# Query variance in one matmul a block after an add on GpSimd, and the key look-up of both key sets in half precision

## The chip, the cores and the metric

One core of a Trainium2 chip runs the whole program. The metric is the device time of one execution in microseconds (us), the median of several runs. The engines are TensorE (PE in the profile, with PEld for its weight loads), VectorE (DVE), ScalarE (ACT), GpSimd (POOL) and SyncE (SP), which issues most of the transfers.

## What is computed

The reference is one layer of a network on 512 tokens of 1024 numbers: a layer norm, an adaptive modulation, a mixer (pooling and a linear recurrence), and a product-key expert layer (PEER). The change lies in the choice of experts:

```python
q = (hf @ w_q).reshape(T, PEER_HEADS, PEER_DKEY)
q = (q - mean(q)) * rsqrt(var(q) + LN_EPS)
s1 = einsum('thd,nd->thn', q[..., :half], k1)
s2 = einsum('thd,nd->thn', q[..., half:], k2)
v1, i1 = top_k(s1, 16)
v2, i2 = top_k(s2, 16)
cand = (v1[..., :, None] + v2[..., None, :]).reshape(T, 8, 256)
vs, j = top_k(cand, 16)
e = i1[j // 16] * 128 + i2[j % 16]
g = softmax(vs)
out = einsum('tk,tkd->td', g * gelu(einsum('td,tkd->tk', x, u[e])), v[e])
```

There are 8 heads with a query of 256 numbers each, two sets of 128 keys, and 16 x 16 candidates of which 16 are kept. The kernel centres the query weights beforehand, so the variance of a query is the mean of its 256 squares.

## The kernel before, in words

All 128 x 128 experts are computed densely for the first 384 tokens (three of four blocks of 128), as 128 tiles of 128 experts: each tile is 24 matmuls of 384 columns (lines 982 to 984, the helper `thrice`, which splits each factor in a high and a low part and multiplies three times). The weights of the chosen experts are scattered into a dense gate. The last 128 tokens gather their rows instead.

The order of work is written out by hand, engine by engine, and semaphores tie the engines together. Around the change it is as follows.

**Queries.** TensorE makes the query of a head in two halves of 24 matmuls each, `queries(h)`. ScalarE reads each half out of its bank twice, as a copy `qT` (line 790) and as a square `sq` (line 791). Once the matmuls of head h+1 are issued, TensorE makes `scores` of head h: 8 matmuls of queries by keys (line 1126), then the variance (line 1130): for each of 4 blocks, two matmuls of one column, the two halves of the squares by a column of 1/256, summed in the bank. In the trace each of these matmuls is two records. ScalarE then reads the scores out (line 802).

**Queue of GpSimd in this stage.** For each head it makes the low parts of two weight pieces (`lo_weights`, line 574), from the fourth head on behind a centring of weights (`centre`, line 592). Then follow the low parts of the expert tiles (`split_u`, line 616, two instructions a tile), of which tiles 2 to 17 come with a scale or a shift of the residual (`affine`, lines 566 and 569).

**Routing on VectorE.** `route(h)` does, per head and in order: the 16 largest of both score lists in 4 blocks (lines 1586 to 1597), a cast of their positions (line 1615), the candidate sums, the 16 largest candidates, integer work that gives the two places `ka` and `kb` of each choice (lines 1625 to 1632), and the look-up of the keys at these places (lines 1634 to 1641): two comparisons with 0 to 15, two products with the positions, two sums over 16. Each of these six works on 128 x 1024 single-precision numbers. `step` links a result to the next instruction by a semaphore. The eight heads follow one another without a pause, and the softmax follows them.

**The turn.** TensorE works on expert tiles 0 to 34 meanwhile. In tile 34, after 6 of its 8 chunks, it waits for the softmax (`s_wt`) and for all keys (`s_e1e2`) and transposes them for the scatter (line 1184, 9 transposes). ScalarE's exponential (line 843) stands in its queue behind the readout of tile 32; GpSimd waits for the picks of the last block before the low part of tile 35. Then TensorE finishes tile 34, does tile 35, and begins 24 scatter steps (lines 1195 and 1197), each with one expert tile. In these VectorE makes the half-precision one-hot tables (lines 1692 and 1698) and the low part of the tile (line 1685).

Of the kernel before, what the change touches and what calls it, by code (L numbers as in the profile page):

```python
# [8 lines left out]
F16 = mybir.dt.float16  # L9
U32 = mybir.dt.uint32  # L10
I32 = mybir.dt.int32
ACT = mybir.ActivationFunctionType
AX = mybir.AxisListType


P = 128
D = 1024
KD = D // P
S = 512
TB = S // P  # L20
# [7 lines left out]
H = 8  # L28
DK = 256
NK = 128  # L30
K = 16
PICKS = H * K
# [94 lines left out]
def build(nc, x, cols, rows, consts, ada_w, w_in, w_out, wq, pool_w, wa, wx, k1t, k2t, ut, u, v, out):  # L127
    ctx = ExitStack()
    with ctx:
# [3 lines left out]
        def sem(name):  # L133
            return ctx.enter_context(nc.semaphore(name))
# [77 lines left out]
        def carve(spec):  # L212
            at, got = 0, []
            for shape in spec:
# [26 lines left out]
        (qT, sq, keys, e1, e2, wt, vs, s_all, s_val, s_pos, s_posf, cand, c_val, c_idx, dec, eq_a, eq_b,  # L241
# [3 lines left out]
             (TB * K, K), (TB * K, K), (4, TB * H)])  # L245

# [72 lines left out]
        s_fin = [sem(f"output{n}_ready") for n in range(TB)]  # L319
        s_wthi, s_wtlo = sem("weights_hi_ready"), sem("weights_lo_ready")  # L320
# [223 lines left out]
        def _(pool):  # L544
# [58 lines left out]
            pool.dma_start(keys[:, 1, :], k2t).then_inc(s_keys, 16)  # L603
            for h in range(1, H):
                if h == 4:
                    pool.wait_ge(s_centre, 4)
                if h >= 4:
                    centre(h)
                if h > 1:
                    lo_weights(NZ + 2 * h)  # L610
                lo_weights(NZ + 2 * h + 1)

# [7 lines left out]
            split_u(0, 1)  # L620
            pool.wait_ge(s_wtlo, NZ + 2 * H)
# [317 lines left out]
        def _(pe):  # L939
# [178 lines left out]
            def scores(par, h, first, var_at):  # L1118

                pe.wait_ge(s_qev, h * 2 + 2)  # L1120
                if not first:
                    pe.wait_ge(s_sev, h * 2 - 2)
                for tb in range(TB):
                    for half in range(2):
                        at = (tb % 2) * DK + half * NK
                        pe.matmul(bank[(2, 5)[par] + tb // 2][:, at:at + NK],
                                  qT[:, par, half, tb * P:(tb + 1) * P], keys[:, half, :], start=True, stop=True)
                for tb in range(TB):
                    for half in range(2):
                        mm = pe.matmul(bank[4][:, var_at(tb)], sq[:, par, half, tb * P:(tb + 1) * P], mean_col,  # L1130
                                       start=(half == 0), stop=(half == 1))
                mm.then_inc(s_smm, 1)
# [151 lines left out]
        def _(ve):  # L1284
# [317 lines left out]
            ka, kb, low = dec[:, 4, :], dec[:, 5, :], dec[:, 6, :]  # L1602
            iota16 = iota[:, 0:K].unsqueeze(1).to_broadcast([P, TB * K, K])
# [3 lines left out]
            def route(h):  # L1607
# [5 lines left out]
                last.then_inc(s_routed, 1)  # L1613
                ve.wait_ge(s_routed, h + 1)
                ve.tensor_copy(s_posf, s_pos.bitcast(U32))
# [18 lines left out]
                ve.tensor_tensor(eq_b, kb.unsqueeze(2).to_broadcast([P, TB * K, K]), iota16, ALU.is_equal)  # L1634
                step(ve.tensor_tensor(eq_a, ka.unsqueeze(2).to_broadcast([P, TB * K, K]), iota16, ALU.is_equal))  # L1635
                ea = eq_a.rearrange("p (t j) a -> p t j a", t=TB)
                eb = eq_b.rearrange("p (t j) a -> p t j a", t=TB)
                ve.tensor_tensor(ea, ea, s_posf[:, 0].unsqueeze(2).to_broadcast([P, TB, K, K]), ALU.mult)  # L1638
                step(ve.tensor_tensor(eb, eb, s_posf[:, 1].unsqueeze(2).to_broadcast([P, TB, K, K]), ALU.mult))  # L1639
                ve.tensor_reduce(e1[:, :, h * K:(h + 1) * K], ea, AX.X, ALU.add)  # L1640
                ve.tensor_reduce(e2[:, :, h * K:(h + 1) * K], eb, AX.X, ALU.add).then_inc(s_e1e2, 1)
# [150 lines left out]
            for c in range(split, early_end):  # L1792
                split_u(0, c)
                n = c - split
# [156 lines left out]
```

## Time and profile before

| what | value |
|---|---|
| median of 3 runs | 1442.37 us (1441.28 to 1442.58) |
| time of the profiled execution | 1443.12 us |
| its span | 1441.3 us |
| PE busy | 1412.3 us, 98% of the span |
| DVE busy | 1239.7 us, 86% |
| ACT busy | 589.5 us, 41% |
| POOL busy | 556.1 us, 39% |
| mean granted clock of TensorE | 0.989 |
| chain that ended last, by engine | PE 70%, DVE 24%, DMA 2%, ACT 2%, issue 1% |

The span is that of one profiled execution, from its first to its last instruction; 1.8 us of that execution's time lie outside it. The chain is followed back from the last instruction, at each step to what released it. A busy engine may still hold others up or be held up for a few microseconds, and such places are found in the waits and in the timeline of an engine.

### The profile page before, as it was taken

The page shows a single profiled execution, that of the slowest core. Times are in us where ns is not written, and L with a number is a line of the kernel's source. Part 1 is how long each engine was busy: PE and PEld are TensorE (multiplying, and loading weights), DVE is VectorE, ACT ScalarE, POOL GpSimd, SP SyncE. Part 2 cuts the span into 40 slices and gives each one's busy share as a digit, 9 for nine tenths or more (in the row PEclk, how much of TensorE's full clock was granted, in tenths as well). Part 3 has the DMA queues.
Part 4 walks back from the last instruction along what each step waited for, and adds up shares of the span by engine and source line. Part 5 has one row for each costly group of instructions (what it writes and reads, how often), then busy time and mean ns, then how long its engine had stood idle before and what let it go on. Part 6 is the DMA issues. An engine that isn't in the chain of part 4 may idle for free.

```text
span 1441.3 us, 20694 instructions
## 1 busy us (share of the span) xinstructions
PE 1412.3 (98%) x7503; PEld 1234.6 (86%) x7503; DVE 1239.7 (86%) x2019; ACT 589.5 (41%) x693; POOL 556.1 (39%) x389
## 2 busy tenths in 40 slices
PE   7999989999998999999999999999999999999997
PEld 6775478899998999998888888888888888888886
DVE  6988969999998999756888888888798888888889
ACT  3561263333334888843333333333333333333331
POOL 0100224549864000002445555454456555554500
PEclk7899999999999999999999999999999999999999
DMA  9824450025565799998999999999999999999961
GB/s 382 326 117 175 146 193 1 1 76 167 174 224 168 263 284 301 290 350 332 371 355 353 375 355 370 355 367 367 349 374 367 371 356 369 381 356 367 353 227 59
DMA packets 159566, 402.34 MB, mean 279 GB/s; under 512 B 11632, under 2 KB 79344, under 8 KB 156432
## 3 DMA queue, kind: packets, MB, share of 16 engines
q1 hardware_dynamic: 120928, 262.17, 51.7%
q0 software_dynamic: 38288, 139.08, 25.4%
q8 instruction: 34, 0.56, 0.2%
q10 hardware_dynamic: 288, 0.29, 0.1%
q14 instruction: 28, 0.23, 0.0%
HBM read 359.56 MB, written 41.94 MB: 279 GB/s over the span
## 4 chain that ended last, share of the span: by engine, by line
PE 70%; DVE 24%; DMA 2%; ACT 2%; issue 1%; SPq 0%; DVEq 0%; ACTq 0%
PE bank L982 22%; PE bank L983 22%; PE bank L984 21%; DVE arena L1597 2%; DVE arena L1589 2%; DMA wbuf<-ada_w_dram 2%; PE bank L1195 2%; PE bank L1197 2%; DVE arena L1594 1%; DVE arena L1586 1%; DVE arena L1638 1%; DVE arena L1591 1%; DVE arena L1639 1%; PE bank L1071 1%; DVE arena L1635 1%
## 5 line engine op out<-in xcount | busy, mean ns | idle before, releaser
L982 PE MATMUL bank<-h_lo,u_hi 128*128 128x384 f32 (+1 forms) x1256 | 438.9, 349 | 2.0 <-POOL u_lo L616 1.9
L983 PE MATMUL bank<-h_hi,u_lo 128*128 128x384 f32 (+1 forms) x1256 | 433.4, 345 | 0.0
L984 PE MATMUL bank<-h_hi,u_hi 128*128 128x384 f32 (+1 forms) x1256 | 433.4, 345 | 0.0
L983 PE MATMUL bank<-v_hi,w_lo 128*128 128x512 f32 x744 | 294.6, 396 | 0.0
L982 PE MATMUL bank<-v_lo,w_hi 128*128 128x512 f32 x744 | 292.1, 393 | 0.3 <-DVE w_lo L1735 0.3
L984 PE MATMUL bank<-v_hi,w_hi 128*128 128x512 f32 x744 | 290.4, 390 | 0.0
L982 PEld LDWEIGHTS bank<-h_lo,u_hi 128*128 128x128 f32 x1256 | 236.5, 188 | 14.0 <-ACT arena L819 2.2
L876 ACT ACTIVATE v_hi<-v_raw 128x2048 fp32r<-128x2048 f32 x62 | 119.0, 1919 | 311.7 <-PE bank L984 301.7
L983 PEld LDWEIGHTS bank<-h_hi,u_lo 128*128 128x128 f32 x1256 | 236.5, 188 | 11.3 <-issue 0.5
L984 PEld LDWEIGHTS bank<-h_hi,u_hi 128*128 128x128 f32 x1256 | 236.3, 188 | 9.5
L1729 DVE TENSOR_TENSOR v_lo<-v_raw,v_hi 128x2048 fp32r<-128x2048 f32 x62 | 142.8, 2303 | 110.5 <-ACT v_hi L876 109.0
L811 ACT ACTIVATE u_hi<-u_raw 128x1024 fp32r<-128x1024 f32 x128 | 135.2, 1057 | 126.2 <-PE bank L984 126.2
L641 POOL DMA_INDIRECT quad<-v_dram,pick_at x86 | 130.7, 1520 | 114.2 <-DVE picked L1756 98.0
L641 POOL DMA_INDIRECT quad<-u_dram,pick_at x84 | 118.0, 1405 | 129.7 <-DVE quad L1748 87.4
L982 PEld LDWEIGHTS bank<-v_lo,w_hi 128*128 128x128 f32 x744 | 139.7, 188 | 32.1 <-DVE w_lo L1735 0.6
L984 PEld LDWEIGHTS bank<-v_hi,w_hi 128*128 128x128 f32 x744 | 139.8, 188 | 31.5
L983 PEld LDWEIGHTS bank<-v_hi,w_lo 128*128 128x128 f32 x744 | 139.6, 188 | 28.3
L641 POOL DMA_INDIRECT first_rows<-u_dram,pick_at x44 | 60.3, 1371 | 252.8 <-DVE w_raw L1722 177.9
L1685 DVE TENSOR_TENSOR u_lo<-u_raw,u_hi 128x1024 fp32r<-128x1024 f32 x92 | 112.2, 1220 | 21.3 <-ACT u_hi L811 15.8
L616 POOL TENSOR_TENSOR u_lo<-u_raw,u_hi 128x512 fp32r<-128x512 f32 x72 | 103.4, 1457 | 46.5 <-ACT u_hi L811 40.3
L1756 DVE SCALAR_TENSOR_TENSOR picked<-quad,pick_g,picked 128x1024 f32<-128x1024 f32 x86 | 110.0, 1279 | 1.6
L1748 DVE SCALAR_TENSOR_TENSOR quad<-quad,h_nat 128x1024 f32<-128x1024 f32 x84 | 101.9, 1219 | 0.0
(246 smaller groups left out, 1815.1 us busy)
## 6 DMA issues: line engine op xcount, KB each, us to landing
u_raw<-ut_dram SPq DMA_DIRECT2D x128, 512.0 KB, 5.7
v_raw<-v_dram SPq DMA_DIRECT2D x64, 1024.0 KB, 7.2
gate_in<-gates_dram SPq DMA_DIRECT2D x64, 384.0 KB, 7.2
wbuf<-ada_w_dram SPq DMA_DIRECT2D x6, 2048.0 KB, 11.3
early_dram<-arena SPq DMA_DIRECT2D x64, 192.0 KB, 2.4
gates_dram<-wbuf SPq DMA_DIRECT2D x12, 1024.0 KB, 7.1
gates_dram<-arena SPq DMA_DIRECT2D x12, 1024.0 KB, 7.4
w_raw<-early_dram SPq DMA_DIRECT2D x64, 192.0 KB, 5.3
```

What stands on the lines that cost most here:

```text
L616: pool.tensor_tensor(u_lo[:, c % GT, ks], u_raw[:, c % RT, ks], u_hi[:, c % GT, ks].bitcast(F32), ALU.subtract).then_inc(done, 1)
L641: pool.indirect_dma_start(row_buf(n), None, of, bass.IndirectOffsetOnAxis(ap=pick_at[:, k:k + 1], axis=0)).then_inc(s_rows_of[n % NBUF], 16)
L811: act.activation(u_hi[:, c % GT], u_raw[:, c % RT], ACT.Copy).then_inc(s_uhi, 1)
L876: act.activation(v_hi[:, c % 2], v_raw[:, c % 2 * 2:c % 2 * 2 + 2, :], ACT.Copy).then_inc(s_vhi, 1)
L982: pe.matmul(out, a_hi, b_lo, start=(k == 0), stop=False)
L983: pe.matmul(out, a_lo, b_hi, start=False, stop=False)
L984: return pe.matmul(out, a_hi, b_hi, start=False, stop=(k == n - 1))
L1195: pe.matmul(bank[q][:, t * P:(t + 1) * P], onehot[b][:, 1, pair, :, at], gate[b][:, 0, pair, :, at], start=True, stop=False)
L1685: ve.tensor_tensor(u_lo[:, c % GT], u_raw[:, c % RT], u_hi[:, c % GT].bitcast(F32), ALU.subtract).then_inc(s_ulo, 1)
L1729: ve.tensor_tensor(v_lo[:, c % 2], v_raw[:, c % 2 * 2:c % 2 * 2 + 2, :], v_hi[:, c % 2].bitcast(F32), ALU.subtract).then_inc(s_vlo, 1)
L1748: ve.scalar_tensor_tensor(out=rows_of, in0=rows_of, scalar=1.0, in1=h_nat[:, :], op0=ALU.mult, op1=ALU.mult, accum_out=dots[:, k:k + 1]).t ...
L1756: ve.scalar_tensor_tensor(out=picked[:, :], in0=rows_of, scalar=pick_g[:, k:k + 1], in1=picked[:, :], op0=ALU.mult, op1=ALU.add).then_inc( ...
```

## The change

Two edits. In the first, GpSimd adds the two halves of a head's squares in place (`sum_squares`), and TensorE makes the variance of each block with one matmul instead of two, behind a new semaphore. In the second, the look-up of the keys of both sets is done together on half-precision numbers laid out in pairs: one comparison and one product on 2048 numbers, then three adds that halve the list of 16 (1024, 512 and 256 numbers), and a last add (128 numbers) that writes single precision. The arrays `e1` and `e2` lie side by side and are written through one view, `e_both`.

```diff
+        e_both = arena[:, 2 * 2 * S + 2 * 2 * S + 2 * NK:][:, 0:2 * TB * PICKS].rearrange("p (m n) -> p m n", m=2 * TB)
...
+            def sum_squares(h):
+
+                pool.wait_ge(s_qev, 2 * h + 2)
+                pool.tensor_tensor(sq[:, h % 2, 0], sq[:, h % 2, 0], sq[:, h % 2, 1], ALU.add).then_inc(s_sqsum, 1)
+
             for h in range(1, H):
...
                 lo_weights(NZ + 2 * h + 1)
+                sum_squares(h - 1)
...
             split_u(0, 0)
             split_u(0, 1)
+            sum_squares(H - 1)
             pool.wait_ge(s_wtlo, NZ + 2 * H)
...
+                pe.wait_ge(s_sqsum, h + 1)
                 for tb in range(TB):
-                    for half in range(2):
-                        mm = pe.matmul(bank[4][:, var_at(tb)], sq[:, par, half, tb * P:(tb + 1) * P], mean_col,
-                                       start=(half == 0), stop=(half == 1))
+                    mm = pe.matmul(bank[4][:, var_at(tb)], sq[:, par, 0, tb * P:(tb + 1) * P], mean_col,
+                                   start=True, stop=True)
...
-            ka, kb, low = dec[:, 4, :], dec[:, 5, :], dec[:, 6, :]
-            iota16 = iota[:, 0:K].unsqueeze(1).to_broadcast([P, TB * K, K])
+            ka, kb, low = (dec[:, 4, :].bitcast(F16)[:, 0:TB * K], dec[:, 4, :].bitcast(F16)[:, TB * K:], dec[:, 6, :])
+            lists, pairs = 2 * TB, K // 2
+            place_of = dec[:, 4, :].bitcast(F16)
+            place = place_of.rearrange("p (g t) -> p g t", t=2)
+            place_key = dec[:, 7, 0:K].bitcast(F16).rearrange("p (a t) -> p a t", t=2)
+            pos_twice = pos_at.rearrange("p a t k -> p (a t k)").bitcast(F16).rearrange("p (a t) -> p a t", t=2)
+            found, told = (a.rearrange("p n k -> p (n k)").bitcast(F16).rearrange("p (g a t) -> p g a t", a=K, t=2)
+                           for a in (eq_a, eq_b))
...
+                if h == 0:
+                    ve.tensor_copy(place_key, iota[:, 0:K].unsqueeze(2).to_broadcast([P, K, 2]))
                 ve.wait_ge(s_routed, h + 1)
-                ve.tensor_copy(s_posf, s_pos.bitcast(U32))
+                ve.tensor_copy(pos_twice, s_pos.rearrange("p a t k -> p (a t k)").bitcast(U32).unsqueeze(2)
+                               .to_broadcast([P, lists * K, 2]))
...
-                ve.tensor_tensor(eq_b, kb.unsqueeze(2).to_broadcast([P, TB * K, K]), iota16, ALU.is_equal)
-                step(ve.tensor_tensor(eq_a, ka.unsqueeze(2).to_broadcast([P, TB * K, K]), iota16, ALU.is_equal))
-                ea = eq_a.rearrange("p (t j) a -> p t j a", t=TB)
-                eb = eq_b.rearrange("p (t j) a -> p t j a", t=TB)
-                ve.tensor_tensor(ea, ea, s_posf[:, 0].unsqueeze(2).to_broadcast([P, TB, K, K]), ALU.mult)
-                step(ve.tensor_tensor(eb, eb, s_posf[:, 1].unsqueeze(2).to_broadcast([P, TB, K, K]), ALU.mult))
-                ve.tensor_reduce(e1[:, :, h * K:(h + 1) * K], ea, AX.X, ALU.add)
-                ve.tensor_reduce(e2[:, :, h * K:(h + 1) * K], eb, AX.X, ALU.add).then_inc(s_e1e2, 1)
+                step(ve.tensor_tensor(found, place.unsqueeze(2).to_broadcast([P, lists * pairs, K, 2]),
+                                      place_key.unsqueeze(1).to_broadcast([P, lists * pairs, K, 2]), ALU.is_equal))
+                step(ve.tensor_tensor(told.rearrange("p (m j) a t -> p m j (a t)", m=lists),
+                                      found.rearrange("p (m j) a t -> p m j (a t)", m=lists),
+                                      pos_twice.rearrange("p (m a) t -> p m (a t)", m=lists).unsqueeze(2)
+                                      .to_broadcast([P, lists, pairs, 2 * K]), ALU.mult))
+                for w in (K // 2, K // 4, K // 8):
+                    step(ve.tensor_tensor(told[:, :, 0:w], told[:, :, 0:w], told[:, :, w:2 * w], ALU.add))
+                ends = [told[:, :, n, :].rearrange("p (m j) t -> p m j t", m=lists) for n in range(2)]
+                ve.tensor_tensor(e_both[:, :, h * K:(h + 1) * K].rearrange("p m (j t) -> p m j t", t=2),
+                                 ends[0], ends[1], ALU.add).then_inc(s_e1e2, 1)
```

Two places show how the queues stand. The line numbers are each program's own. On GpSimd, from the first low weight piece behind the key loads to the first expert tiles, before (`u_lo<-wbuf` is a low weight piece, `wbuf<-wbuf,hmean` a centring, `u_lo<-u_raw` a low expert tile):

```order
23 L574 TENSOR_TENSOR u_lo<-wbuf,u_hi 128x1024 x5
24 L592 TENSOR_TENSOR wbuf<-wbuf,hmean 128x8x256
25 L574 TENSOR_TENSOR u_lo<-wbuf,u_hi 128x1024 x2
...
30 L592 TENSOR_TENSOR wbuf<-wbuf,hmean 128x8x256
31 L574 TENSOR_TENSOR u_lo<-wbuf,u_hi 128x1024 x2
32 L616 TENSOR_TENSOR u_lo<-u_raw,u_hi 128x512 x6
33 L566 TENSOR_TENSOR xt<-xt,row_g 128x512
```

and now (`arena<-arena` of line 610 is the add of the squares):

```order
23 L577 TENSOR_TENSOR u_lo<-wbuf,u_hi 128x1024
24 L610 TENSOR_TENSOR arena<-arena 128x512
25 L577 TENSOR_TENSOR u_lo<-wbuf,u_hi 128x1024 x2
26 L610 TENSOR_TENSOR arena<-arena 128x512
27 L577 TENSOR_TENSOR u_lo<-wbuf,u_hi 128x1024 x2
28 L610 TENSOR_TENSOR arena<-arena 128x512
29 L595 TENSOR_TENSOR wbuf<-wbuf,hmean 128x8x256
...
39 L577 TENSOR_TENSOR u_lo<-wbuf,u_hi 128x1024 x2
40 L610 TENSOR_TENSOR arena<-arena 128x512
41 L625 TENSOR_TENSOR u_lo<-u_raw,u_hi 128x512 x4
42 L610 TENSOR_TENSOR arena<-arena 128x512
43 L625 TENSOR_TENSOR u_lo<-u_raw,u_hi 128x512 x2
```

An add of the squares stands behind the second weight piece of each head, ahead of the next centring; the last stands behind the low parts of expert tiles 0 and 1.

On VectorE, the look-up of one head with the instruction ahead of it, before (names in brackets are the semaphores waited for):

```order
224 L1632 TENSOR_TENSOR arena<-arena 128x64 [waits route_step]
225 L1634 TENSOR_TENSOR arena<-arena,cst 128x1024 [waits route_step]
226 L1635 TENSOR_TENSOR arena<-arena,cst 128x1024
227 L1638 TENSOR_TENSOR arena<-arena 128x1024 [waits route_step]
228 L1639 TENSOR_TENSOR arena<-arena 128x1024
229 L1640 TENSOR_REDUCE arena<-arena 128x4x16 [waits route_step]
230 L1641 TENSOR_REDUCE arena<-arena 128x4x16
```

and now (the size is that of the output):

```order
225 L1651 TENSOR_TENSOR arena<-arena 128x64 [waits route_step]
226 L1653 TENSOR_TENSOR arena<-arena 128x2048 [waits route_step]
227 L1655 TENSOR_TENSOR arena<-arena 128x2048 [waits route_step]
228 L1660 TENSOR_TENSOR arena<-arena 128x64x16 [waits route_step]
229 L1660 TENSOR_TENSOR arena<-arena 128x64x8 [waits route_step]
230 L1660 TENSOR_TENSOR arena<-arena 128x64x4 [waits route_step]
231 L1662 TENSOR_TENSOR arena<-arena 128x8x16 [waits route_step]
```

Six instructions stand for six; all of the new ones have two inputs, and each waits for the one ahead of it.

## Rows read from the trace of the kernel before

**Rows 1.** The page, part 1: busy us, share of span, instructions.
```profile
PE 1412.3 (98%) x7503; PEld 1234.6 (86%) x7503; DVE 1239.7 (86%) x2019; ACT 589.5 (41%) x693; POOL 556.1 (39%) x389
```

**Rows 2.** Waits of PE: line, releaser: us in total, times, longest us.
```profile
PE bank L1184 <- issue: 3.6, 1, 3.6
PE bank L982 <- POOL u_lo L616: 1.9, 1, 1.9
```

**Rows 3.** Timeline of PE, variance of heads 0 and 6: start us, us, instruction.
```profile
213.77 1.84 PE L1130 MATMUL bank<-cst,arena 128*128 128x1 f32 x16
215.48 0.49 PE L982 MATMUL bank<-h_lo,u_hi 128*128 128x512 f32 x1
...
300.85 1.84 PE L1130 MATMUL bank<-cst,arena 128*128 128x1 f32 x16
302.79 0.41 PE L982 MATMUL bank<-h_lo,u_hi 128*128 128x384 f32 x1
```

**Rows 4.** Timeline of POOL, queries to tiles, and tiles with affine.
```profile
274.68 3.61 POOL L592 TENSOR_TENSOR wbuf<-wbuf,hmean 128x2048 f32<-128x2048 f32 x1
...
286.86 2.37 POOL L574 TENSOR_TENSOR u_lo<-wbuf,u_hi 128x1024 fp32r<-128x1024 f32 x1 [2.97 <-ACT u_hi L697]
301.37 5.02 POOL L616 TENSOR_TENSOR u_lo<-u_raw,u_hi 128x512 fp32r<-128x512 f32 x4 [12.14 <-ACT u_hi L811]
308.52 2.60 POOL L616 TENSOR_TENSOR u_lo<-u_raw,u_hi 128x512 fp32r<-128x512 f32 x2 [2.13 <-ACT u_hi L811]
...
349.47 4.36 POOL L616 TENSOR_TENSOR u_lo<-u_raw,u_hi 128x512 fp32r<-128x512 f32 x2 [0.37 <-ACT u_hi L811]
353.79 2.27 POOL L569 TENSOR_TENSOR xt<-xt,row_b 128x512 f32<-128x512 f32 x1
356.02 3.50 POOL L616 TENSOR_TENSOR u_lo<-u_raw,u_hi 128x512 fp32r<-128x512 f32 x2
```

**Rows 5.** Chain that ended last, look-ups of heads 2 and 7: start us, us, what.
```profile
290.97 1.23 DVE arena L1634
...
296.98 1.12 DVE arena L1641
...
442.32 1.23 DVE arena L1634
...
451.49 1.13 DVE arena L1641
```

**Rows 6.** Groups by line, DVE: busy us, mean ns | idle us.
```profile
L1692 DVE TENSOR_TENSOR arena<-arena 128x2048 f16<-128x2048 f16 x24 | 28.4, 1221 | 0.0
L1615 DVE CAST arena<-arena 128x128 f32<-128x128 uint32 x8 | 2.5, 313 | 0.3
```

**Rows 7.** Timeline of PE at the turn.
```profile
452.83 0.33 PE L983 MATMUL bank<-h_hi,u_lo 128*128 128x384 f32 x1
453.00 0.34 PE L984 MATMUL bank<-h_hi,u_hi 128*128 128x384 f32 x1
...
457.80 1.54 PE L1184 MATMUL bank<-cst,arena 128*128 128x128 f32 x6 [0.35 <-ACT arena L819]
...
465.14 0.24 PE L1195 MATMUL bank<-arena 128*128 128x128 f16 x1
...
467.01 0.44 PE L982 MATMUL bank<-h_lo,u_hi 128*128 128x384 f32 x1
```

**Rows 8.** Windows: us, busy us (instructions) PE, PEld, DVE, ACT, POOL; PEclk, DMA, GB/s.
```profile
458.00:464.00 6.00, 6.00 (x30) 6.00 (x30) 3.94 (x5) 2.54 (x6) 3.06 (x4) 0.77 0.69 206
```

**Rows 9.** Timeline of ACT at the turn.
```profile
447.63 1.28 ACT L843 ACT_TABLE_LOAD   x1
454.37 0.63 ACT L843 ACTIVATE arena<-arena 128x512 f32<-128x512 f32 x1 [5.45 <-DVE arena L1657]
```

**Rows 10.** Timeline of DVE behind the turn.
```profile
459.95 0.36 DVE L1676 CAST arena<-arena 128x384 f16<-128x384 f32 x1 [2.53 <-ACT arena L852]
...
465.74 1.22 DVE L1685 TENSOR_TENSOR u_lo<-u_raw,u_hi 128x1024 fp32r<-128x1024 f32 x1
```

More of the change, by code:

```diff
@@ L239, in build @@
         part = arena[:, ARENA - 2 * CHUNK_C:].rearrange("p (b n) -> p b n", b=2)
-        (qT, sq, keys, e1, e2, wt, vs, s_all, s_val, s_pos, s_posf, cand, c_val, c_idx, dec, eq_a, eq_b,
+        (qT, sq, keys, e1, e2, wt, vs, s_all, s_val, s_pos, pos_at, cand, c_val, c_idx, dec, eq_a, eq_b,
          pk) = carve(
@@ L245, in build @@
              (TB * K, K), (TB * K, K), (4, TB * H)])
+        e_both = arena[:, 2 * 2 * S + 2 * 2 * S + 2 * NK:][:, 0:2 * TB * PICKS].rearrange("p (m n) -> p m n", m=2 * TB)
+        assert 2 * TB * K * K == 2 * (TB * K * K)
         s_of = ([s_all[:, 0], s_all[:, 1], arena[:, ARENA - TB * DK:].rearrange("p (t n) -> p t n", t=TB), s_all[:, 2]]
@@ L319, in build @@
         s_fin = [sem(f"output{n}_ready") for n in range(TB)]
+        s_sqsum = sem("query_squares_summed")
         s_wthi, s_wtlo = sem("weights_hi_ready"), sem("weights_lo_ready")
```

## Prediction

> **What bounds the kernel now.** I read the page's busy shares first: TensorE is busy for 98% of the span [rows 1]. Only two things can then shorten the run: less work on TensorE, or fewer of its few idle microseconds. Its waits show two that matter here: 3.6 us in front of the transposes of the turn, and 1.9 us for a low expert tile from GpSimd [rows 2]. The chain of waits says what stands behind the first. VectorE's routing is on it for all eight heads, and the last look-up ends at 451.49 + 1.13 = 452.62 us [rows 5]. ScalarE's exponential waits 5.45 us for the shifted values [rows 9] and TensorE waits for the softmax after that. So routing is late by a few microseconds against tile 34, and nowhere else in front of the turn does TensorE wait for it. Behind the turn TensorE is full again to within a few microseconds, so time won before it stays won.
>
> **The variance on TensorE.** One head's 16 records take 215.48 - 213.77 = 1.71 us [rows 3]. Half of them goes: 0.86 us a head. For seven heads that is 6.0 us off the path. For head 6 I count nothing. Its 16 records stand ahead of expert tile 0, and the next matmul starts 302.79 - 300.85 = 1.94 us after the first of them, 0.23 us later than for head 0: the low part of tile 0, which GpSimd began at 301.37 us, is already what it waits for [rows 3, 4], and the edit does not speed that up. Bounds: 5.1 us if another head loses its share, 6.9 us if all eight count.
>
> **The add on GpSimd.** Eight instructions of 128 x 512 with two inputs. The nearest row is the low expert tile, 5.02 / 4 = 1.26 us each [rows 4]. I cost them at nothing on the path, for these covers. From variance to variance a head takes (300.85 - 213.77) / 6 = 14.5 us [rows 3]. GpSimd has two weight pieces of 2.4, a centring of 3.6 and now 1.3 us in it, 9.7 us [rows 4]. The squares of head 6 are added behind the piece that ends at 286.86 + 2.37 = 289.23 us, so by about 290.5 us, and their variance begins at 300.85 us: 10 us to spare [rows 3, 4]. Queued behind each add are the next centring and the next weight piece, which come 1.3 us later; the pieces' idle of about 3 us for ScalarE [rows 4] takes most of that up. The last add falls into the 2.13 us that GpSimd waits ahead of tile 2 [rows 4]. If the cover were gone, the price would be 1.26 us a head.
>
> **The look-up on VectorE.** Alone, in head 2, the old six take from 290.97 to 298.10 us, 7.1 us; in head 7, among GpSimd's instructions, from 442.32 to 452.62 us, 10.3 us [rows 5]. For the new ones, the half-precision one-hot tables have the same shape and pairing: 2048 numbers in 1.22 us [rows 6], so 2.44 us for comparison and product. The three adds and the last one have no row. Below lies the rate of the tables without a fixed part, (1024 + 512 + 256 + 128) / 2048 x 1.22 = 1.1 us; above lies one number in 1.2 ns, that of the comparison [rows 5], with the 0.31 us of the cast of 128 numbers as the floor of each [rows 6], 2.5 us. I take a line between table and cast, 0.73 + 0.49 + 0.37 + 0.31 = 1.9 us, since the first two are nearest to the tables. Sum 4.3 us, a saving of 2.8 us in a head that is alone. The cast of positions doubles, at most 0.3 us more [rows 6], and one small cast comes once. That leaves at least 2.5 x 8 = 20 us over the heads.
>
> How much is needed? TensorE and with it ScalarE come to the turn 6.0 us earlier, and the values are 5.45 us late now [rows 9], so 11.5 us; 0.86 us comes from routing beginning earlier. The need is 10.6 us, 1.3 us a head. I expect it met, and what is over is worth nothing: ScalarE takes the exponential behind tile 32 whatever comes earlier.
>
> **The turn.** With the softmax there, TensorE goes on after 453.17 us (in the times of before) with 9 transposes at about 0.107 us (the pace of the variance's records, the nearest row [rows 3]) and 6 + 24 matmuls at 0.17 us [rows 7]: 453.17 + 1.0 + 5.1 = 459.3 us for the first scatter matmul, which came at 465.14 us [rows 7]. So 5.9 us are lost now: the waits, and matmuls at the low clock, since the granted clock was 0.77 in the 6 us behind the wait [rows 8]. What is late next is VectorE's preparation of the scatter. From the second lot of transposes at 457.80 us to its first cast at 459.95 us lie 2.15 us, and 7.06 us more to the matmul at 467.01 us that needs its low part of tile 36 [rows 7, 10]. Starting the second lot at about 453.5 us gives 453.5 + 2.15 + 7.06 = 462.7 us instead of 467.01: **4.3 us won**, 1.6 given back. I take 4.3; the upper bound is 5.9.
>
> **GpSimd among the expert tiles.** In tiles 2 to 17 it makes a low tile and an affine piece per tile, 3 x 1.26 = 3.8 us of TensorE's 24 x 0.17 = 4.1 us. In head 4's look-up its instructions stretched to 4.36, 2.27 and 3.50 us where 2.5, 1.3 and 2.5 are usual [rows 4], 3.8 us in all, and TensorE's 1.9 us of waiting came of it [rows 2]. The new look-up holds GpSimd for about as long (4.3 us against the old four two-input instructions' 4 x 1.15), but heads come closer together and two may fall into this stage. Bounds: 1.9 us won if none does, 3.8 us lost if two more do. I take 1.0 us lost.
>
> **Sum.** 6.0 + 4.3 - 1.0 = 9.3 us. The profiled execution took 1443.12 us (span 1441.3 and 1.8 around it), so its like would take 1433.8; against the median of 1442.37 us, 0.8 below that execution, **1433.1 us**.
>
> **Rivals.**
> First, more: GpSimd's wait vanishes and the scatter's preparation keeps up. 6.0 + 5.9 + 1.9 = 13.8 us, 1428.6 us. For it speaks that the add instructions are short; against it that heads 3 to 5 still meet the busy stage.
>
> Second, GpSimd becomes the bound among the expert tiles. All six new look-up instructions have two inputs, where two of the old six were sums with one. If three heads fall into tiles 2 to 17 and each costs TensorE what a stretch of 3.8 us less 0.9 of slack costs, 2.9 us, the wait is 8.7 us for 1.9: 6.0 + 4.3 - 6.8 = 3.5 us won, 1438.9 us. For it speak the stretched rows [rows 4]; against it that the same total of VectorE time is held.
> The Trainium skill, "SBUF — State Buffer", section "Who interferes with whom", states that VectorE instructions with two SBUF inputs and GpSimd instructions that read SBUF shut each other out for a whole instruction. The stretched rows agree. By that rule alone every new instruction may stand behind one of GpSimd's.
> Six waits of 1.26 us on 4.3 us would make a look-up 11.9 us, longer than the 10.3 us of before, where GpSimd never rests; with at most three such heads and 2.5 us saved in the five others, 12.5 - 4.8 = 7.7 us are saved where 10.6 are needed, and the turn would keep about 3 us of its wait. I leave that inside this rival's time.
>
> Third, the half-precision look-up is no faster. At one number in 1.12 ns, 2048 take 2.3 us, the six 2 x 2.3 + 2.5 = 7.1 us, just what the old take. Then VectorE ends where it did but for 0.86 us, and all that TensorE saves is spent waiting at the turn: 1441.5 us, no change. Against it stand the tables' 1.22 us [rows 6].
> The Trainium skill, "Vector Engine (DVE) Microarchitecture Reference", section "Performance modes", reports that a two-source instruction on 2-byte numbers fell to the single rate when one input re-read one element as its innermost step. Here the innermost step is a pair of neighbours, as in the tables, whose row shows the double rate; by the rule the place to look is the last add, whose output is single precision.
>
> Fourth, slower: the new wait in front of the variance. If the squares come late, TensorE stands with the next head's queries queued behind. It decides once an add ends after the eight key matmuls; each head would then pay an add held by a VectorE instruction, 1.26 + 1.15 = 2.4 us, 19.3 us over the eight, against 6.9 + 4.3 won: 8 us lost, 1450.5 us. For it speaks only that the add is queued behind two weight pieces; against it stand 10 us of slack.
>
> **How the numbers follow.** Forecast 0.66, more 0.11, GpSimd as the bound 0.14, no faster look-up 0.06, late squares 0.03. The range 1428.5 to 1438.0 holds the forecast with its bounds (6.9 + 5.9 - 1.0 = 11.8 us won; 5.1 + 4.3 - 3.8 = 5.6 us won), the better case and half of the second rival. About 0.2% (2.9 us) is what a measurement can tell from no change: faster is below 1439.5 us. That is the forecast, the better case and some 0.10 of the second rival, 0.87; no change is its rest and the third, 0.10; slower is 0.03.
>
> **What would show it.** Right: 64 records of the variance at about 0.86 us a head with no idle before them; the look-up at 4 to 5 us alone; the exponential without its 5.45 us of waiting; the granted clock near 1 behind the turn; scatter starting 10 to 11 us earlier; a wait for GpSimd's low tiles of 1 to 4 us. Wrong: an idle TensorE in front of the variance, a comparison of over 2 us in a head that is alone, or the waits for low tiles above 6 us.

## The result: 1446.7 us, slower by 4.4

The changed kernel takes 1446.69 us (median of 8 runs, 1446.05 to 1448.23), the kernel before 1442.32 us beside it (8 runs, 1441.13 to 1443.39): a ratio of 1.0033, 95% interval 1.0024 to 1.0041. The forecast of 1433.1 us and its range to 1438.0 us are missed, and on the other side.

In the lines of the changed kernel the comparison of a look-up is line 1653, the product 1655, the three adds 1660, the last add 1662; on GpSimd a weight piece is line 577, the add of the squares 610, a centring 595. The page's part 1, which answers to [rows 1]:

```profile
PE 1405.0 (97%) x7439; PEld 1226.1 (85%) x7439; DVE 1244.5 (86%) x2020; ACT 590.0 (41%) x693; POOL 563.4 (39%) x397
```

TensorE does 32 matmuls less (64 records, two to a matmul) and is busy 7.3 us less, and yet the span grew from 1441.3 to 1444.7 us. Its waits (columns as in [rows 2]) say where this went:

```profile
PE bank L1194 <- DVE arena L1684: 14.2, 1, 14.2
...
PE bank L992 <- POOL u_lo L625: 1.7, 3, 1.0
```

The timeline of TensorE at the turn, and below it that of ScalarE:

```profile
445.68 0.34 PE L994 MATMUL bank<-h_hi,u_hi 128*128 128x384 f32 x1
460.21 2.41 PE L1194 MATMUL bank<-cst,arena 128*128 128x128 f32 x9 [14.19 <-DVE arena L1684]
```

```profile
440.31 1.28 ACT L853 ACT_TABLE_LOAD   x1
457.64 0.63 ACT L853 ACTIVATE arena<-arena 128x512 f32<-128x512 f32 x1 [16.05 <-DVE arena L1679]
```

TensorE comes to the turn at 446.0 us, 7.3 us earlier than before [rows 7], where the variance had promised 6.0, and stands there for 14.2 us. The exponential waits 16.05 us, where it waited 5.45 [rows 9]. Routing is taken here from the first maximum of head 0 to the instruction behind the last look-up. Its two ends in the kernel before, and below them now:

```profile
216.77 1.65 DVE L1586 MAX8 arena<-arena 128x8 f32<-128x128 f32 x8 [10.20 <-ACT arena L802]
...
452.54 0.34 DVE L1651 RECIPROCAL arena<-arena 128x32 f32<-128x32 f32 x1
```

```profile
215.67 1.65 DVE L1596 MAX8 arena<-arena 128x8 f32<-128x128 f32 x8 [8.06 <-ACT arena L812]
...
455.81 0.35 DVE L1673 RECIPROCAL arena<-arena 128x32 f32<-128x32 f32 x1
```

It ends 3.3 us later, and the span is 3.4 us longer. All that TensorE won is spent waiting for VectorE.

Routing did not lose time everywhere. By VectorE's timeline (a head begins with its first maximum) the first four heads, which run beside the projection of the queries and the first expert tiles, took 127.9 us in place of 108.7; the last four 112.2 in place of 127.1. So the question is what held VectorE in the first four heads. The chain that ended last, in the look-up of head 0 (start, us, what):

```profile
236.06 1.24 DVE arena L1653
...
237.32 3.31 DVE arena L1655
...
240.65 0.70 DVE arena L1660
...
241.38 2.64 DVE arena L1660
...
244.04 1.28 DVE arena L1660
...
245.34 3.58 DVE arena L1662
```

and GpSimd's timeline in the same microseconds:

```profile
236.08 3.45 POOL L577 TENSOR_TENSOR u_lo<-wbuf,u_hi 128x1024 fp32r<-128x1024 f32 x1 [1.17 <-ACT u_hi L707]
241.33 2.40 POOL L577 TENSOR_TENSOR u_lo<-wbuf,u_hi 128x1024 fp32r<-128x1024 f32 x1 [1.80 <-ACT u_hi L707]
243.68 1.48 POOL L610 TENSOR_TENSOR arena<-arena 128x512 f32<-128x512 f32 x1
245.12 3.65 POOL L595 TENSOR_TENSOR wbuf<-wbuf,hmean 128x2048 f32<-128x2048 f32 x1
```

Each of VectorE's held instructions ends just behind one of GpSimd's. The product comes out 1.1 us, a little under its own 1.24, behind the end of the first piece (239.53 us), which the comparison had held back in its turn; the second add 0.3 us behind the second piece (244.02 and 243.73), the third 0.2 us behind the add of the squares (245.32 and 245.16), and the last add, 128 results, 0.15 us behind the centring (248.92 and 248.77). Head 7's look-up runs while TensorE stands and GpSimd is out of work, and shows what the same six cost alone:

```profile
451.57 1.24 DVE arena L1653
...
452.83 1.24 DVE arena L1655
...
454.09 0.70 DVE arena L1660
...
454.82 0.44 DVE arena L1660
...
455.28 0.30 DVE arena L1660
...
455.60 0.29 DVE arena L1662
```

From 451.57 to 455.81 us are 4.24 us, against 12.78 for head 0. Over all eight heads (instructions by line: duration in ns, min/median/max, first and last start):

```profile
L1655 DVE TENSOR_TENSOR arena<-arena x8: 1225/2200/3295, 237.3 to 452.8; 128x2048 f16<-128x2048 f16 x8
```

```profile
L1660 DVE TENSOR_TENSOR arena<-arena x24: 292/1270/2756, 240.7 to 455.3; 128x1024 f16<-128x1024 f16 x8, 128x512 f16<-128x512 f16 x8, 128x256 f16<-128x256 f16 x8
```

```profile
L1662 DVE TENSOR_TENSOR arena<-arena x8: 293/1263/3579, 245.3 to 455.6; 128x128 f32<-128x128 f16 x8
```

An add that takes 0.29 us alone takes 1.26 us in the middle of the cases and 3.58 at worst. That is not its own work but the length of one whole instruction of GpSimd (1.26, 2.4 or 3.6 us). The sums with one input that the old look-up ended with, in the kernel before:

```profile
L1641 DVE TENSOR_REDUCE arena<-arena x8: 1208/1209/1210, 243.9 to 451.4; 128x64 f32<-128x1024 f32 x8
```

were held in no head.

### The profile page after: what moved, and what is told of

It is laid out like the page before. It is cut to its first block, busy times and chain, and to the rows that moved or that the text cites. A ratio compares the mean times of both kernels' runs of the same rounds, so it can differ in the third digit from the quotient of the medians.

```text
span 1444.7 us, 20575 instructions
## 1 busy us (share of the span) xinstructions
PE 1405.0 (97%) x7439; PEld 1226.1 (85%) x7439; DVE 1244.5 (86%) x2020; ACT 590.0 (41%) x693; POOL 563.4 (39%) x397
## 4 chain that ended last, share of the span: by engine, by line
PE 70%; DVE 24%; DMA 2%; ACT 2%; issue 1%; SPq 0%; DVEq 0%; ACTq 0%
PE bank L992 22%; PE bank L993 21%; PE bank L994 21%; DVE arena L1660 2%; DVE arena L1607 2%; DVE arena L1599 2%; DMA wbuf<-ada_w_dram 2%; PE bank L1205 2%; PE bank L1207 2%; DVE arena L1604 1%; DVE arena L1596 1%; DVE arena L1655 1%; DVE arena L1601 1%; DVE arena L1653 1%; PE bank L1081 1%
## 5 line engine op out<-in xcount | busy, mean ns | idle before, releaser
L992 PEld LDWEIGHTS bank<-h_lo,u_hi 128*128 128x128 f32 x1256 | 236.4, 188 | 14.2 <-issue 1.5
L993 PEld LDWEIGHTS bank<-h_hi,u_lo 128*128 128x128 f32 x1256 | 236.5, 188 | 11.3 <-issue 0.5
```

The costliest lines, as they stand in the source:

```text
L992: pe.matmul(out, a_hi, b_lo, start=(k == 0), stop=False)
L993: pe.matmul(out, a_lo, b_hi, start=False, stop=False)
```

## The experiments

Theory H: VectorE's instructions with two inputs and GpSimd's hold each other for a whole instruction; the new look-up has six such for four, and the adds of the squares put more of GpSimd's in their way. Rivals: the halves of the change lose by something of their own (late squares, a slow operation), or the start of routing against GpSimd's rhythm decides by chance.

Read from the traces of the main kernels: routing as above, the sum of its eight look-ups, and what is held, which is routing less 8 times a head that is alone (24.0 us with the old look-up, 21.2 with the new, 21.7 with one sum). Each routing time is that of one profiled execution; the ratio is to the kernel before taken beside each.

| kernel | routing us | look-ups us | held us | time us | ratio to before, 95% |
|---|---|---|---|---|---|
| before | 235.8 | 74.2 | 43.8 | 1442.3 | |
| after | 240.1 | 71.2 | 70.5 | 1446.7 | 1.0024 to 1.0041 |
| variance part alone | 247.9 | 85.2 | 55.9 | 1455.1 | 1.0066 to 1.0100 |
| look-up part alone | 227.9 | 55.7 | 58.3 | 1436.3 | 0.9940 to 0.9973 |
| after, one sum for the adds | 207.8 | 46.9 | 34.2 | 1429.7 | 0.9890 to 0.9923 |

**The variance part alone** (the old look-up):

```diff
+                sum_squares(h - 1)
...
-                    for half in range(2):
-                        mm = pe.matmul(..., sq[:, par, half, ...], mean_col, start=(half == 0), stop=(half == 1))
+                    mm = pe.matmul(..., sq[:, par, 0, ...], mean_col, start=True, stop=True)
```

> The first edit alone: GpSimd adds the squares and TensorE makes the variance with one matmul a block; the look-up is the old one. Theory A (routing on VectorE ends last at the turn, and an instruction of VectorE that reads two arrays stands behind a running GpSimd instruction): the adds put more GpSimd work beside routing, the old look-up has four instructions that can be held, and what TensorE saves is spent waiting at the turn. Routing about 236 us long as before, give or take 3, time 1440 to 1445 us. Theory B (the adds on GpSimd are what made the change slower, the look-up helps): routing 243 us or longer, time above 1447 us.

**The look-up part alone** (the change without the add of the squares, with the two matmuls a block):

```diff
-                sum_squares(h - 1)
...
-                    mm = pe.matmul(..., sq[:, par, 0, ...], mean_col, start=True, stop=True)
+                    for half in range(2):
+                        mm = pe.matmul(..., sq[:, par, half, ...], mean_col, start=(half == 0), stop=(half == 1))
```

> The second edit alone: the half-precision look-up of both key sets; the variance is the old one. Theory A: the six instructions with two inputs are held as often as GpSimd runs, so routing is not shorter than before by more than 4 us, and may be longer; time 1438 to 1446 us. Theory B (the look-up helps, the adds hurt): routing shorter by 15 us or more, the wait at the turn gone, time below 1438 us.

Measured: the variance part loses 12 us by itself, as theory B said, and the look-up part wins 6. Theory A fell in both runs. Of the look-up part theory B had the time and the turn right, but routing fell by 7.9 us where B wanted 15: the new look-up helps, and is held more all the same. TensorE's wait at the turn in the variance part alone:

```profile
PE bank L1192 <- DVE arena L1670: 19.2, 1, 19.2
```

In the look-up part alone no wait stands ahead of the 9 transposes of the turn (line 1186 there); what is left is 0.7 us further on, ahead of a scatter matmul (line 1197) that waits for VectorE's one-hot tables:

```profile
451.66 1.14 PE L1186 MATMUL bank<-cst,arena 128*128 128x128 f32 x9
...
457.88 0.24 PE L1197 MATMUL bank<-arena 128*128 128x128 f16 x1
```

```profile
PE bank L1197 <- DVE arena L1712: 0.7, 1, 0.7
```

With these two look-ups the effects add up: the variance part brings routing 12.1 us with the old one (235.8 to 247.9) and 12.2 with the new (227.9 to 240.1). It is no fixed price, though, as a run below with another look-up shows. The look-up part saves 22.4 us of work alone (8 times 2.8) and is held 14.5 us more, so 7.9 us of routing are left.

**One sum for the four adds** (the change, with the whole sum over 16 places in one instruction with one input):

```diff
-                for w in (K // 2, K // 4, K // 8):
-                    step(ve.tensor_tensor(told[:, :, 0:w], told[:, :, 0:w], told[:, :, w:2 * w], ALU.add))
-                ve.tensor_tensor(e_both[...], ends[0], ends[1], ALU.add).then_inc(s_e1e2, 1)
+                ve.tensor_reduce(e_both[...].rearrange("p m (j t) -> p m j t", t=2),
+                                 told.rearrange("p (m j) a t -> p m j t a", m=lists), AX.X, ALU.add).then_inc(s_e1e2, 1)
```

> The change with its three adds and the last add replaced by one sum over 16 with one input, 2048 numbers, some 2.2 us by the old sums' 1.21 us for 1024. Alone the look-up is then 1.22 + 1.22 + 2.2 = 4.7 us, longer than the 4.3 us of the change. Theory A: only two instructions of the look-up can be held, so it takes 5 to 8 us in each head where the change took 8 to 13, routing ends 15 to 25 us earlier than in the change, the exponential does not wait, and the time is 1432 to 1437 us. Theory C (the length of the instructions decides, holds are the same whatever the count): no better than the change, 1446 us or more.

Alone this look-up is longer (4.72 us for 4.24), and yet routing falls by 32.3 us, to 207.8, and the time to 1429.67 us (ratio 0.9907). Both are better than theory A allowed; theory C fell. The sum's row, and TensorE's waits (line 1205 is a scatter matmul):

```profile
L1659 DVE TENSOR_REDUCE arena<-arena x8: 2285/2286/2287, 241.1 to 421.7; 128x128 f32<-128x2048 f16 x8
```

```profile
PE bank L992 <- POOL u_lo L625: 1.0, 1, 1.0
...
PE bank L1205 <- DVE arena L1717: 0.7, 1, 0.7
```

Eight records within 2 ns of each other, in the same stage in which four short adds took up to 3.6 us each; no wait for the softmax is left. H holds here, and this version beats both kernels. The same again:

> The change with one sum over 16, taken again beside the runs above and in five rounds, as the version that beat both kernels: 1428.5 to 1431 us, ratio to the kernel before 0.990 to 0.992 by every theory that takes routing off the path.

1430.24 us, ratio 0.9911 (0.9894 to 0.9927); routing again took 207.8 us.

**One add, then the sum over 8 places:**

```diff
+                step(ve.tensor_tensor(told[:, :, 0:K // 2], told[:, :, 0:K // 2], told[:, :, K // 2:], ALU.add))
-                                 told.rearrange(...)
+                                 told[:, :, 0:K // 2].rearrange(...)
```

> The change with its first add kept (1024 numbers, 0.70 us alone) and one sum over the 8 left in place of the other three adds (1024 numbers, 1.21 us). Alone 1.22 + 1.22 + 0.70 + 1.21 = 4.35 us. Theory A: three instructions can be held in place of six, routing 10 to 20 us shorter than in the change and up to 8 us longer than with the one sum; the turn's wait is gone all the same, 1432 to 1438 us. Theory C: as the change, 1446 us.

Routing 212.5 us, 4.7 more than with the one sum, for one instruction that can be held; that is 27.6 us less than in the change, more than theory A's 20. The time, 1430.40 us (0.9896 to 0.9929), doesn't show the 4.7, since routing is off the path by then.

**The one sum with the old variance:**

> The look-up with one sum over 16 and the old variance, no adds on GpSimd. With the adds this look-up gave 1429.7 us and no wait at the turn. Theory A: routing is shorter still without the adds (200 us or less by their 12 us elsewhere), but nothing waits for it, and TensorE has its 16 records a head back: 1434 to 1438 us, 5 to 7 us slower than with the adds. Rival (the sum is what wins, the variance edit gives nothing on TensorE): 1429 to 1431 us.

Routing 204.7 us; 1436.76 us (0.9938 to 0.9972). Against 1429.7 to 1430.2 with the variance in one matmul, that part is worth 6.5 to 7.1 us, once routing is off the path, so the rival fell. Routing was to be 200 us or less and is not: with this look-up the variance part brings it 3.1 us (204.7 to 207.8), not 12.

The rest asks why the variance part holds routing by 12 us with the other two look-ups. **The adds without TensorE's gain** (the variance part alone, with the summed squares multiplied twice):

```diff
+                    for half in range(2):
+                        mm = pe.matmul(bank[4][:, 64 * half:][:, var_at(tb)], sq[:, par, 0, ...], mean_col, ...)
```

> The old look-up, GpSimd's adds of the squares as in the first edit, but TensorE does as much as before: of its two matmuls a block one makes the variance and the other a copy of it in columns that nothing reads. Theory A1 (the adds themselves, 1.29 us each behind a weight piece and ahead of a centring, hold routing): routing is 245 to 250 us as with the first edit alone (247.9), time 1450 to 1456 us. Theory A2 (what hurts is that a faster TensorE moves the weight pieces and centrings closer together and under other parts of routing): routing 234 to 239 us, time 1440 to 1445 us.

Routing 236.8 us, 1444.0 us (0.9998 to 1.0017): the adds alone cost 1.0 us of routing.

**TensorE's gain without the adds** (the kernel before with the first half of the squares alone; the second is left out of the variance):

> The old look-up, no adds on GpSimd, and one matmul a block: the variance is made of the first half of the squares alone, the second half is left out. Theory A1: routing as before (236 us, give or take 3), TensorE waits longer at the turn, time 1439 to 1443 us. Theory A2: routing 245 us or longer, time above 1449 us.

Routing 232.2 us, 1438.72 us (0.9965 to 0.9984): this costs routing nothing either. Theory A1 fell in the run before, A2 in this one: only both together cost the 12 us.

**A later start.** One, two or four sums over 1024 numbers ahead of head 0's routing, in the changed kernel, and two in the variance part alone:

```diff
+                for _ in range(N if h == 0 else 0):
+                    step(ve.tensor_reduce(dec[:, 6, 0:1], s_all[:, 0].rearrange("p t n -> p (t n)"), AX.X, ALU.add))
```

> The whole change, with one idle sum (1024 numbers, one input, about 1.2 us) on VectorE ahead of the first head's routing, so that routing starts 1.2 us later against GpSimd's pieces. Theory P (how long routing takes hangs on which of its two-input instructions fall on GpSimd's runs of weight piece, add and centring, so it moves by several microseconds with the start): routing without the idle sum changes from 240.1 us by 3 us or more, up or down; time anywhere from 1436 to 1452 us. Theory S (each edit brings a fixed sum of holds): routing 240 us give or take 1.5, time 1.2 us above the change, 1446.5 to 1449 us.

> As the run before with two idle sums, 2.4 us. Theory P: another routing time, 3 us or more from 240.1 or from the run before. Theory S: time 2.4 us above the change, 1448 to 1450 us.

> With four idle sums, 4.8 us. Theory P: at least one of the three delays makes the run faster than the change itself, though VectorE does more; this one 1438 to 1455 us. Theory S: 4.8 us above the change, 1450 to 1453 us.

> The first edit alone (old look-up, GpSimd's adds, 1455.1 us, routing 247.9 us) with two idle sums, 2.4 us, ahead of the first head's routing. Theory P: the 12 us that adds and faster TensorE cost together, while neither alone cost more than 1.5, are a matter of alignment and part by 3 us or more: 1445 to 1452 us, or above 1460. Theory S: 2.4 us later, 1456.5 to 1459 us.

Routing took 238.8, 241.3 and 238.5 us for 240.1, and 251.8 for 247.9; the times were 1446.09, 1450.55, 1450.18 and 1460.85 us (1.0018 to 1.0037, 1.0039 to 1.0073, 1.0038 to 1.0071 and 1.0109 to 1.0142). Neither theory came out as written. In the changed kernel routing moved by less than the 3 us that theory P wanted, and the 0.6 us by which one delay was faster lie within the spread of the runs. In the variance part alone it moved by 3.9 us, to above 1460, as P said. Theory S fell there, and in the changed kernel the delays of 1.2, 2.4 and 4.8 us came out as 0.6 us less, 3.9 and 3.5 us more. So the start is worth up to 4 us of routing, and differences below that should not be read as a cause. But none of these starts gave the 12 us back, and two of the four made routing longer.

**The add between the weight pieces**, instead of behind both:

```diff
+                sum_squares(h - 1)
                 lo_weights(NZ + 2 * h + 1)
-                sum_squares(h - 1)
```

> The variance part alone (old look-up), with the add of the squares queued between the two weight pieces of a head instead of behind them, so that GpSimd's longest row without a pause is add and piece (3.7 us) and piece and centring (6.0 us, as in the kernel before), not 7.3 us. Theory B (a row of piece, add and centring without a pause is what holds routing): routing falls from 247.9 to at most 240 us, the time from 1455 to 1447 us or less. Theory L (the load on GpSimd in a shorter turn of the heads counts, wherever the add stands): routing 245 to 250 us, 1453 to 1457 us.

Routing 247.9 us, 1453.48 us (1.0052 to 1.0086): where the add stands among the pieces doesn't matter to routing. Theory B fell, L's figures came true.

**Adds of half the length:**

> The variance part alone (old look-up) with adds of 256 of the 512 columns (the second halves of the other columns' squares are left out): 0.65 us for 1.29. Theory L (load): routing in the middle between that with no adds and TensorE as fast, 232.2, and that with whole adds, 247.9: 238 to 242 us. Theory B (a row without a pause): the row is 6.6 us for 7.3, so most of the loss stays, 244 us or more. Theory J (chance of the alignment): anything from 230 to 250 us without order.

Routing 236.8 us, 1443.66 us (0.9990 to 1.0011). B fell again, and it is less than L said: beside TensorE's gain alone (232.2 us) whole adds cost 15.7 us of routing and half adds 4.6, so the loss doesn't grow evenly with the load.

**Short centrings**, in the variance part alone, in the kernel before, and in the whole change:

```diff
-                pool.tensor_tensor(w, w, hmean[:, h, :].unsqueeze(2).to_broadcast([P, KD, DK]), ALU.add
+                pool.tensor_tensor(w[:, 0:1], w[:, 0:1], hmean[:, h, 0:1].unsqueeze(2).to_broadcast([P, 1, DK]), ALU.add
```

> The variance part alone (old look-up) with centrings of 256 columns in place of 2048: 7 of 8 key chunks of the query weights stay without their mean. A centring then takes about 0.7 us for 3.6. If the 3.6 us centrings are what the adds and the shorter turn make routing meet more often, routing is within 3 us of the kernel before with the same short centrings; if they are not, it stays 8 us or more above it.

> The kernel before with centrings of 256 columns in place of 2048 (7 of 8 key chunks of the query weights stay without their mean): the mate of the run ahead of it. Routing falls from 235.8 us by 2 to 10 us, since 2.9 us of GpSimd a head go; the time follows by at most 6 us, what the turn waits.

> The whole change, with centrings of 256 columns in place of 2048 (7 of 8 key chunks of the query weights stay without their mean). With the old look-up the short centrings took the variance part's loss of 12.1 us of routing away but for 0.4 us. Theory C (adds, a faster TensorE and 3.6 us centrings hold routing only together): routing is as with the new look-up alone, 227.9 us, less what short centrings bring by themselves, 4 us: 222 to 229 us, and the time 1432 to 1437 us. Rival N (the six two-input instructions of the new look-up are held whatever the centrings): routing 235 us or more, 1440 us or more.

GpSimd's row of the variance part alone, one turn of the heads, with whole centrings and then with short ones:

```profile
230.05 1.29 POOL L608 TENSOR_TENSOR arena<-arena 128x512 f32<-128x512 f32 x1
231.30 3.61 POOL L593 TENSOR_TENSOR wbuf<-wbuf,hmean 128x2048 f32<-128x2048 f32 x1
236.07 3.45 POOL L575 TENSOR_TENSOR u_lo<-wbuf,u_hi 128x1024 fp32r<-128x1024 f32 x1 [1.17 <-ACT u_hi L705]
```

```profile
230.11 1.29 POOL L608 TENSOR_TENSOR arena<-arena 128x512 f32<-128x512 f32 x1
231.36 0.62 POOL L593 TENSOR_TENSOR wbuf<-wbuf,hmean 128x256 f32<-128x256 f32 x1
236.00 2.99 POOL L575 TENSOR_TENSOR u_lo<-wbuf,u_hi 128x1024 fp32r<-128x1024 f32 x1 [4.03 <-ACT u_hi L705]
```

The pause behind the centring grows from 1.17 to 4.03 us, and routing takes 232.1 us with the adds (1437.98 us, 0.9950 to 0.9980) and 231.7 without (1439.23 us, 0.9965 to 0.9991): of 12.1 us of loss 0.4 are left. In the whole change routing takes 222.6 us in place of 240.1, and the time is 1430.91 us (0.9888 to 0.9945), 1 us below the range of theory C; rival N is out. The turn's wait of 14.2 us is gone, and what is left is the wait ahead of a scatter matmul:

```profile
PE bank L1205 <- DVE arena L1720: 0.7, 1, 0.7
```

So the runs show that the variance part's loss, with the old look-up, needs three things at once: GpSimd's whole adds, the shorter turn of the heads on TensorE (13.6 us for 14.5), and centrings of 3.6 us. Take any one away and routing is within 1.1 us of the same kernel without the variance part, or below it.

What stays open is the step from these three to the 12 us. GpSimd's two pauses in a turn (in brackets) shrink. In the kernel before they are 3.2 and 2.8 us; in the variance part alone the first is 1.2 us, as shown above, and the second 1.8. The kernel before, then the variance part alone:

```profile
237.94 2.57 POOL L574 TENSOR_TENSOR u_lo<-wbuf,u_hi 128x1024 fp32r<-128x1024 f32 x1 [3.19 <-ACT u_hi L697]
243.32 2.38 POOL L574 TENSOR_TENSOR u_lo<-wbuf,u_hi 128x1024 fp32r<-128x1024 f32 x1 [2.81 <-ACT u_hi L697]
```

```profile
241.31 2.81 POOL L575 TENSOR_TENSOR u_lo<-wbuf,u_hi 128x1024 fp32r<-128x1024 f32 x1 [1.78 <-ACT u_hi L705]
```

The pauses don't decide it by themselves: with the one sum they are the same 1.2 and 1.8 us, and the loss is 3.1. By heads, the variance part alone loses 11.8 us in heads 0 and 1, among the weight pieces, and 11.3 in heads 2 and 3, and the last four give 10.9 back. For the second share the traces offer a reason. Between its last work for the queries and the first expert tile GpSimd pauses for 12.1 us in the kernel before and for 9.9 in the variance part alone. In the kernel before, head 2's look-up begins in that pause, at 290.97 us, and nothing holds it [rows 4, 5]. In the variance part alone, heads 0 and 1 being late, it begins at 303.12 us, when the pause is over and GpSimd is among the expert tiles:

```profile
284.62 1.28 POOL L608 TENSOR_TENSOR arena<-arena 128x512 f32<-128x512 f32 x1
295.79 5.04 POOL L623 TENSOR_TENSOR u_lo<-u_raw,u_hi 128x512 fp32r<-128x512 f32 x4 [9.89 <-ACT u_hi L819]
```

```profile
303.12 2.21 DVE L1642 TENSOR_TENSOR arena<-arena,cst 128x1024 f32<-128x1024 f32 x1
```

In each of the seven runs whose routing is more than 2 us longer than in the kernel before, head 2's look-up begins behind this pause; in all others it begins before the pause ends. That is read from the traces and not shown, since no run moved head 2's look-up alone, and why heads 0 and 1 lose their 11.8 us only with all three together stays unexplained.

## Why the prediction was wrong, and where it was right

**Wrong: the look-up's saving.** "At least 2.5 x 8 = 20 us over the heads ... I expect it met." The alone price was right: 4.24 us in head 7 for the 4.3 worked out, comparison and product 1.24 us each for 1.22. But a look-up was alone in one head of eight; the sum went from 74.2 to 71.2 us, 3.0 saved where 20 were counted and 10.6 needed. Without the variance part it fell to 55.7, and 7.9 us of routing were won. The step took the saving of a head that is alone, 2.8 us, for every head. Yet its own row of head 7 [rows 5] already showed 3.2 us of holding on four instructions that can be held, and the new look-up offers six.

**Wrong: the add on GpSimd at nothing.** "I cost them at nothing on the path, for these covers." The covers are those of TensorE's path, and there the step was right: no idle time stands ahead of the variance. But VectorE's routing, which the same text had put on the chain for all eight heads, shares the stage with these adds, and no cover was sought for it. The cover also set GpSimd's 9.7 us against a turn of 14.5 us, which the edit itself shortens to 13.6. Together with that shorter turn the adds cost 12.1 us of routing; in a turn of 14.5 us they cost 1.0.

**Wrong with these: the turn.** 4.3 us were to be won and the wait grew by 10.6 us instead (14.2 for 3.6), since routing was late. The mechanism was right: in the look-up part alone and with the one sum, where routing is in time, the wait is gone. Its size was then too low: in the look-up part alone, with TensorE's variance as before, the granted clock is 1.00 from 452 to 464 us, the first scatter matmul starts at 457.88 us for 465.14 [rows 7], and the time falls by 6 us.

**Right: the variance on TensorE.** 64 records less and 6.0 us for seven heads were forecast. Head 0's eight records, to the next matmul:

```profile
213.57 0.95 PE L1140 MATMUL bank<-cst,arena 128*128 128x1 f32 x8
214.38 0.49 PE L992 MATMUL bank<-h_lo,u_hi 128*128 128x512 f32 x1
```

0.81 us for 1.71 [rows 3], 0.90 us a head and 6.3 for seven. Head 6 gives nothing, as written: its 1.94 us to the next matmul stay. In the time it is 6.5 to 7.1 us, once routing is off the path. The wait for low tiles, 1.7 us, is within the 1 to 4 us forecast.

**The rivals.** None was this case. The second had the mechanism but the wrong place: it gave it to at most three heads among the expert tiles, and to TensorE's low tiles. In the query stage, where it decided, GpSimd's instructions are longer (2.4 and 3.6 us for 1.26). The rule of the Trainium skill, "SBUF — State Buffer", section "Who interferes with whom", that such instructions shut each other out for a whole one, agrees with the trace (the last add 3.58 us behind a centring of 3.65), and its list there, by which a sum with one input never meets GpSimd, agrees too (2285 to 2287 ns). The prediction's working by that rule gave a look-up of 11.9 us, and that it comes near head 0's 12.78 is luck: it counted six waits of 1.26 us, and head 0 had four, of 1.0 to 3.3. But the question was the right one, and should have been asked of all eight heads. The fourth, slower, looked at the same queue for late squares, and squares were not late.

## What to carry to other kernels

Price an instruction on VectorE not by its work alone but by the GpSimd instruction beside which it will be issued. A short one with two inputs may cost a whole one of the neighbour, so of two forms the one with fewer such instructions can win though it is longer alone. Work that is put on an idle GpSimd has to be covered on VectorE's path too, not only on that of the engine that takes its result. Where two engines are within a few microseconds of each other at a meeting point, time won on the one is worth what the other gives.

## What the runs showed of the hardware

In the changed kernel copies and casts with one input are held too, in few heads: the cast of positions (line 1633) took 294 ns in the middle of its eight cases and 3602 at most, the copy of 64 numbers (line 1643) 208 and 3599 ns. The sums of the kernel before and the one sum never were. The same GpSimd piece stretches in turn, from 2.40 to 3.45 us, when a comparison of 1.24 us holds it.
